# Retention output of a two-block layer stack, computed with tokens on partitions instead of features

## The reference

```
for layer in range(DEPTH_2):
    h = rms_norm(x, pre_norm[layer])
    proj = h @ w_in[layer]          # c_b c_c c_x c_z r_q r_k r_v r_z
    ...
    q, k = rotary(r_q), rotary(r_k)
    scores[i, j] = (q_i . k_j) * decay(i - j) / sqrt(128)      (j <= i)
    ret_i = sum_j scores[i, j] * v_j            # written in chunks of 128 tokens
    ret = ret * rsqrt(mean(ret * ret, axis=-1) + 1e-6)         # per token and head
    y_ret = ret * silu(r_z)
    out = concat(y_conv, y_ret) @ w_out[layer]
    x = x + rms_norm(out, post_norm[layer])
```

## Time and profile before

| | |
|---|---|
| median of 3 runs | 2066.09 us (2065.78 to 2068.53) |
| the profiled execution | 2066.39 us, its span in the trace 2064.6 us |
| mean granted TensorE clock | 0.975 of full speed |
| busy: PE, DVE, ACT, POOL | 95%, 55%, 32%, 3% of the span |
| weight loads (PEld) | 84% of the span |
| DMA | 165.52 MB, 80 GB/s over the span |

### The profile page before, as it was taken

The page is one execution under the profiler, slowest core; times in us unless marked ns, Lnnn a source line. Parts: engine busy times, 40 slices in busy tenths (PEclk is TensorE's granted clock), DMA queues, the critical chain, the costliest instruction groups (busy, mean ns, idle before and its releaser), DMA issues.

```text
span 2064.6 us, 30485 instructions
## 1 busy us (share of the span) xinstructions
PE 1969.5 (95%) x11905; PEld 1732.4 (84%) x11905; DVE 1132.6 (55%) x1481; ACT 661.8 (32%) x960; POOL 65.9 (3%) x67
## 2 busy tenths in 40 slices
PE   6999999998989999999799999999978999999997
PEld 6998888888989989989578888888857888888886
DVE  6777786786645535555654554445245555445422
ACT  3123344344324525324422222222222222222222
POOL 1000000001000000000000000000000000000000
PEclk8999999999999999999899999999989999999999
DMA  4221111111222232322222321332222222233231
GB/s 137 94 82 60 44 61 41 61 41 62 82 82 82 81 102 81 102 82 66 77 72 92 91 91 61 102 102 85 98 61 71 91 91 74 78 97 95 92 102 41
DMA packets 159194, 165.52 MB, mean 80 GB/s; under 512 B 2969, under 2 KB 156066, under 8 KB 159155
## 3 DMA queue, kind: packets, MB, share of 16 engines
q1 hardware_dynamic: 156648, 160.73, 24.4%
q10 hardware_dynamic: 2186, 4.20, 0.6%
q0 software_dynamic: 320, 0.07, 0.0%
HBM read 162.88 MB, written 2.10 MB: 80 GB/s over the span
## 4 chain that ended last, share of the span: by engine, by line
PE 53%; issue 40%; DVE 3%; ACT 2%; POOL 1%; DVEq 0%; DMA 0%; ACTq 0%; POOLq 0%
PE acc L373 44%; PE acc L675 2%; PE acc L477 1%; PE tr L709 1%; PE tr L408 1%; POOL pw L315 1%; PE sc L398 1%; PE sc L695 1%; PE tr L549 0%; DVE h L1484 0%; PE sc L515 0%; ACT w_hi L774 0%; DVE ssum L1496 0%; PE tr L547 0%; PE sc L408 0%
## 5 line engine op out<-in xcount | busy, mean ns | idle before, releaser
L1103 DVE TENSOR_TENSOR w_lo<-raw,w_hi 128x2048 fp32r<-128x2048 f32 x150 | 343.2, 2288 | 175.4 <-ACT w_hi L774 173.6
L774 ACT ACTIVATE w_hi<-raw 128x2048 fp32r<-128x2048 f32 x149 | 284.5, 1911 | 355.2 <-PE acc L373 354.5
L373 PE MATMUL acc<-s_lo,w_hi 128*128 128x512 f32 x896 | 359.6, 401 | 19.2 <-DVE s_lo L1488 13.0
L373 PE MATMUL acc<-s_hi,w_lo 128*128 128x512 f32 x896 | 352.8, 394 | 0.0
L373 PE MATMUL acc<-s_hi,w_hi 128*128 128x512 f32 x896 | 352.7, 394 | 0.0
L373 PE MATMUL acc<-n_lo,w_hi 128*128 128x256 f32 x1600 | 339.7, 294 | 12.5 <-DVE n_lo L1131 6.2
L373 PE MATMUL acc<-n_hi,w_hi 128*128 128x256 f32 x1600 | 328.8, 287 | 0.0
L373 PE MATMUL acc<-n_hi,w_lo 128*128 128x256 f32 x1600 | 328.7, 287 | 0.0
L373 PEld LDWEIGHTS acc<-n_lo,w_hi 128*128 128x128 f32 x1600 | 253.2, 191 | 25.2 <-issue 19.9
L373 PEld LDWEIGHTS acc<-n_hi,w_lo 128*128 128x128 f32 x1600 | 254.4, 191 | 0.0
L373 PEld LDWEIGHTS acc<-n_hi,w_hi 128*128 128x128 f32 x1600 | 254.3, 191 | 0.0
(11 more groups left out here) (247 smaller groups left out, 2438.3 us busy)
## 6 DMA issues: line engine op xcount, KB each, us to landing
raw<-in_w_in SPq DMA_DIRECT2D x92, 1024.0 KB, 5.4
raw<-in_w_up SPq DMA_DIRECT2D x22, 1024.0 KB, 5.0
raw<-in_w_out SPq DMA_DIRECT2D x20, 1024.0 KB, 4.9
raw<-in_w_down SPq DMA_DIRECT2D x8, 1024.0 KB, 5.0
raw<-in_w_conv_out SPq DMA_DIRECT2D x4, 1024.0 KB, 5.0
decay<-in_decay ACTq DMA_DIRECT2D x8, 512.0 KB, 3.4
raw<-in_w_down SPq DMA_DIRECT2D x4, 768.0 KB, 4.2
xs<-in_x SPq DMA_DIRECT2D x4, 512.0 KB, 5.3
```

The lines of the kernel that those rows point to most:

```text
L373: last = pe.matmul(acc[jj][:, bank, at_:at_ + n], w[j][:, k, jj * P:(jj + 1) * P], x[:, k0 + k, c:c + n], start=start and k == 0 and p == ...
L774: act.activation(w_hi[j][:, :, :], raw[j][:, :, :], ACT.Copy).then_inc(hi_full[j], 1)
L1103: dve.tensor_tensor(w_lo[j][:, :, :], raw[j][:, :, :], w_hi[j][:, :, :].bitcast(fp32), ALU.subtract).then_inc(lo_full[j], 1)
```

## The change

The roles in retain are exchanged: the decayed scores are stationary in blocks of 128x128, v moves, and the output has tokens on partitions and features along the free dimension. The two heads go to different halves of the PSUM tile tr (ret_at), so the copy into rq between them goes away. The squares' sums over features are now sums along the free dimension: ScalarE squares each block of 128 and adds up in the same instruction (accum_out into es). The reciprocal root of a token is then a value per partition, and VectorE scales the output straight from PSUM into rq. To get back to features on partitions, TensorE transposes four blocks a head (turn) into sc, and VectorE multiplies those by the gate. The column sums and the broadcast leave the loop, and with them their semaphores' counts (bc_l in place of st_l, not shown).

More of the change, by code:

```diff
@@ L74 @@
 LAY_ST = 6
+LAY_BC = 2
 ST_END = ST_LAY + LAYERS * LAY_ST
+BC_END = ST_LAY + LAYERS * LAY_BC
 KINDS = [None, 0, 1, 2, 3]
@@ L190, in build, with st_at, ret_at @@
         tr = ctx.enter_context(nc.psum_tensor("tr", [P, 2, 512], fp32))
+        def st_at(kb):
+            return kb * SEQ - P * (kb * (kb - 1) // 2)
+        def ret_at(hh):
+            return tr[:, 1 - hh, :]
         def scores_at(kb):
@@ L213, in build @@
             "ret_done cy0_full cconv cm_full ch_full c_done post ld_pos o_tr o_cp ss_zero mean_v "
-            "wo_half retm ld_decay trig cpad prep").split()}
+            "wo_half retm ld_decay trig cpad prep turned").split()}
         block = ctx.enter_context(nc.Block())
@@ L651, in _ @@
                 st_l = l * LAY_ST + ST_LAY
+                bc_l = l * LAY_BC + ST_LAY
                 pe.wait_ge(s["ss_full"], l * (2 * KT) + 3 * KT)
@@ L688, in scores_t @@
                             pe.wait_ge(s["qk_full"], l * 16 + i * 4 + 4)
-                            pe.wait_ge(s["rb_full"], st_l + i + 2)
+                            pe.wait_ge(s["rb_full"], bc_l + 2)
                         else:
@@ L1012, in _ @@
                 f_l = l * LAY_F + 2 * B_LAY
-                st_l = l * LAY_ST + ST_LAY
+                bc_l = l * LAY_BC + ST_LAY
                 hi(0, b_l, (acc_full[1], f_l))
                 hi(1, b_l, (acc_full[1], f_l))
-                rstd(st_l, [tr], 0)
+                rstd(bc_l, [tr], 0)
                 for t in range(KT):
@@ L1022, in _ @@
                     square(l * (2 * KT) + 3 * KT, t, h[:, t, META:], (s["h_full"], l * KT + (t + 1)), width=SEQ)
-                act.wait_ge(s["st_bc"], st_l + 2)
+                act.wait_ge(s["st_bc"], bc_l + 2)
                 act.activation(rp[:, :], tr[:, 0, :], ACT.Copy).then_inc(s["rb_full"], 1)
@@ L1034, in _, with square_sums @@
                                   src=acc[jj][:, 0, :])
-                    def copy_ret(hh):
+                    def square_sums(hh):
                         act.wait_ge(s["ro_psum"], hd0 + hh + 1)
-                        act.activation(sq[:, hh, 0:SEQ], tr[:, 1, :], ACT.Square).then_inc(s["ret"], 1)
-                        act.activation(rq[:, hh, :], tr[:, 1, :], ACT.Copy).then_inc(s["ro_full"], 1)
+                        for q in range(NQT):
+                            last = act.activation(sq[:, hh, q * P:(q + 1) * P], ret_at(hh)[:, q * P:(q + 1) * P],
+                                                  ACT.Square, accum_out=es[:, hh, q:q + 1])
+                        last.then_inc(s["ret"], 1)
                     hi_for(0, b1 + 2, f1 + 4)
-                    copy_ret(0)
-                    copy_ret(1)
+                    square_sums(0)
+                    square_sums(1)
                     for jj in range(2):
@@ L1469, in _ @@
                 ss_l = l * (2 * KT) + 3 * KT
-                mean_square(st_l, 4, 1.0 / D, 1e-6)
+                bc_l = l * LAY_BC + ST_LAY
+                mean_square(bc_l, 4, 1.0 / D, 1e-6)
                 start_sum(0)
@@ L1473, in _ @@
                 dve.wait_ge(s["h_zero"], 2)
-                dve.wait_ge(s["rb_full"], st_l + 1)
+                dve.wait_ge(s["rb_full"], bc_l + 1)
                 for t in range(KT + 2):
@@ L1496, in _ @@
                     dve.tensor_tensor(ssum[:, 0:SEQ], ssum[:, 0:SEQ], sq[:, t % 2, 0:SEQ], ALU.add).then_inc(s["ss_full"], 1)
-                mean_square(st_l + 1, 4, 1.0 / D, 1e-6)
+                mean_square(bc_l + 1, 4, 1.0 / D, 1e-6)
                 lo(1, b_l)
@@ L1544, in _ @@
                     lo(0, b1 + 2)
-                    dve.wait_ge(s["rb_full"], st_l + 2)
+                    dve.wait_ge(s["rb_full"], bc_l + 2)
                     scale_z(0)
-                    dve.wait_ge(s["st_sum"], st_l + i + 3)
-                    dve.tensor_tensor(head_ms[:, :], sc[:, 0, 0:8], pp2[:, :], ALU.mult).then_inc(s["hv"], 1)
+                    dve.wait_ge(s["ret"], hd0 + 2)
+                    dve.tensor_tensor(head_ms[:, :], es[:, :, :].rearrange("p a n -> p (a n)"), pp2[:, :],
+                                      ALU.mult).then_inc(s["hv"], 1)
                     dve.wait_ge(s["hv"], l * 4 + i + 1)
@@ L1636, in _ @@
             weigh(0, 3)
-            mean_square(ST_END, 4, 1.0 / D, 1e-6)
+            mean_square(BC_END, 4, 1.0 / D, 1e-6)
             weigh(3, KT)
```

## The result

The changed kernel takes 2109.4 us (median, 2109.21 to 2110.49), the kernel before 2067.11 us in the same comparison (2065.78 to 2068.53). The ratio is 1.0206, with a 95% interval of 1.0188 to 1.0223: 42 us slower, 10 of them more than the sum had.

The account below looks back on a forecast made before the run. TensorE's own queue was taken to bound the retention loop, eight passes of about 56.5 us. Queue gain -20.6, waits +41.2 and clock +11.7 made +32.3 us, so 2098 us, with 8 in 10 for 2086 to 2111.

Parts of the forecast that it names:

- the sum: Over eight passes of the retention loop: -20.6 + 41.2 + 11.7 = +32.3 us, given as 2098 us.
- The queue's gain: TensorE's queue in the loop: sums and broadcast leave, small matmuls and transposes enter; -2.6 us a pass, -20.6 over eight.
- The wait before K: End of each pass: TensorE waits for VectorE to free acc0 behind turn(1); 5.2 or 5.0 us, 41.2 over eight.
- turn(0) costs nothing: Head 0's transposes don't wait for VectorE's scaled output, being covered by queued matmuls with about 4 us left.
- The clock: Behind each wait before K, TensorE runs one stretch at 0.50, losing 1.5 us; 8 x 1.5 = 11.7 us.
- (a): Rival: the wait before K is there but the clock doesn't fall; +20.6, 2087 us; chance 0.09.
- (b): Rival: behind the wait the clock stays down longer, or waits come out longer; +3.0 a pass, 2110 us; chance 0.13.
- the case of one short stretch: Main case: one wait of about 5 us and one slow stretch a pass; 2090 to 2106 us; chance 0.68.
- (c): Rival: TensorE's transposes or small matmuls cost more than their trace spacing; 1.5 a pass for transposes, 2110 us; chance 0.05.
- (d): Rival: K doesn't wait because VectorE frees acc0 in time; only the queue's gain stays, 2045.5 us; chance 0.05.

Follow-up runs that it names:

- both turns together: The changed kernel with the transposes of both heads placed together behind the first tile of Q; 2046.77 us, ratio 0.990 to the kernel before.
- filled version: The changed kernel with 22 useless matmuls of 512 columns between the second turn and K; 2090.17 us, ratio 1.011 to the kernel before.
- turns in the middle of a tile: The changed kernel with both turns behind step four of eight of Q's first tile, gate multiplies ahead of lo; 2047.23 us, ratio 0.9901.
- half filled: The changed kernel with 11 useless matmuls between the second turn and K; 2096.86 us, ratio 1.0134 to the kernel before.
- four steps ahead: The changed kernel with head 1's transposes four steps (12 matmuls) ahead of the end of Q's second tile; 2081.31 us, ratio 1.0061.
- the wait alone: The kernel before, VectorE edited only: head 1's gate multiply waits for both Q tiles, lo made ahead of the multiplies; 2128.75 us, ratio 1.0294.

## Why the prediction was right, point by point

- **The queue's gain.** The forecast was 2.6 us a pass. ScalarE's first copy of v is at 1177.81 and 1234.37 in the kernel before, 56.56 us a pass, and a pass without a wait (both turns together) is 54.00: 2.56 us. The output matmuls of a head, from the changed kernel's timeline, 1078.15 to 1080.31, take 2.16 us against 2.07 and a forecast of 2.12:

```profile
1078.15 2.40 PE L719 MATMUL tr<-rv,st 128*128 128x128 f32 x20
1080.31 0.48 PE L383 MATMUL acc<-s_lo,w_hi 128*128 128x512 f32 x1
```

- **The wait before K.** Forecast 5.2 and 5.0, measured 5.08 to 5.11 and 4.87; 41.2 against 40.3 us. The brackets count from the modelled end of the last record. Counted as the forecast did, from the moment at which K could have issued (1102.20 + 0.35 = 1102.55), the first wait is 5.35, and a pass of the filled version is just that much longer than one without a wait, 59.35 against 54.00. So the sum was a little low here, not high. That it comes from the place of the second turn is shown by four kernels: moved away, it goes; moved by six and by twelve matmuls, it shrinks to 3.7 and 2.3; put into the kernel before, it comes there.
- **turn(0) costs nothing.** No wait stands before it: GpSimd was done with the power at 1089.19, VectorE with the scaled output of both heads at 1092.91, and head 0's turn issued at 1096.27: 3.4 us to spare, against a forecast of about 4.
- **The clock is the term that was mis-sized.** The step was "I take one such stretch a pass: 8 x 1.5 = 11.7 us". In the changed kernel all eight stretches are 6.7 us at 0.50, and 4.8 to 5.6 us of each fall on matmuls; the filled wait prices them at 2.4 us a pass (19 us), which is 7 of the 10 us that the sum lacked. The passes say the same: 1250.77 - 1189.17 = 61.60 us between two copies of v, less the 59.35 of the filled version, whose K starts as late, is 2.25; over the six passes it is 2.2 to 2.6. What led me wrong was taking the length of the stretch from waits of 1.9 and 3.1 us. The trace of the kernel before has a wait of 4.41 us behind dense matmuls, in the first block, and the clock is at 0.50 for 6.7 us there. I didn't use it. The wait nearest in length, 5.09 us until 1018.14, would not have helped, since the clock is at 0.50 before that wait begins:

```profile
510.01 0.78 PE L373 MATMUL acc<-n_lo,w_hi 128*128 128x256 f32 x2 [4.41 <-DVE n_lo L1336]
...
509.10:515.80 6.70, 5.79 (x26) 0.50 0.00 0
...
1012.00:1013.00 1.00, 1.00 (x5) 0.50 0.00 0
```

- **The remainder.** The spans differ by 43.1 us. The first copy of v in the loop is 0.8 us late (1065.52 against 1064.69), and a ScalarE instruction behind the last pass is 41.65 late (1841.26 against 1799.61), so 40.8 us come in between, nearly all of them from the eight passes (8 x 5.1). The 0.8 is a balance of parts outside the change: the changed kernel loses 1.3 us before 898 us and 1.5 in a stretch at 0.50 from 902 to 905 us, and lacks a stretch that the kernel before has at 1058.7. The last 1.5 us are lost at the very end, where the changed kernel's clock is at 0.50 for 6.7 us (2089.8 to 2096.5) and that of the kernel before for 3.3 (2048.5 to 2051.8). That any of this has to do with the change isn't shown.
- **The rivals.** (a) is refuted: the clock fell at each of the eight waits. (b) was what happened to the clock, at 2.4 of its 3.0 us: I gave it 0.13, and 0.68 to the case of one short stretch. The measured 2109.4 lies outside the 2090 to 2106 of that case and inside 2086 to 2111 only because that range took in (b). (c) is refuted by the run without transposes (0.84 us a pass for eight) and by the 2.16 us of the output matmuls. (d), the gain without the wait, isn't what this change does, but 2045.5 was right for it: a kernel with both turns behind Q's first tile has 2046.8.

By the Trainium skill's 275 ns a transpose ("TensorE: Matmul & The Clock Gate", Part 4, PE-mode transpose) the sum would have been an estimated 2110. That is near the measured 2109.4, and for the wrong reason: the runs put a transpose at about 0.1 us of the queue.

The best version that the experiments found is the one with both turns together, from which the one with turns in the middle of a tile can't be told apart: 1% below the kernel before, from the changed kernel by moving one call of four transposes.

## What to carry to other kernels

Ask of each instruction that is put into a full queue not what it takes but who now waits for it, and what stands behind that wait on the other engine. The transposes cost 0.8 us a pass, and the place of half of them cost 7.6: the multiply that waited for them stood in VectorE's queue ahead of the operation that freed TensorE's next accumulator. Where a product alternates between few PSUM tiles, work handed to another engine belongs at least one whole tile ahead of the tile's reuse. And a wait on TensorE should be priced with the clock behind it, here nearly half as much again.

## What the runs showed of the hardware

- The fall of the clock behind a wait isn't a function of its length alone. Waits of 3.08 us (kernel before, second layer) and, in four of eight cases, of 2.35 to 2.59 us (half filled) left it at 1.00, while all eight of 2.1 to 2.4 us (four steps ahead) were followed by a stretch at 0.50. The same wait of 1.94 us at a loop's start was followed by such a stretch in the kernel before and by none in the changed one (1.00 from 1059.5 to 1065.0).
- Waits of 3.5 to 3.7 us were followed by 3.4 or by 6.8 us at 0.50. Those of 4.9 to 5.1 in the changed kernel were always followed by about 6.7, of which 4.8 to 5.6 fell on matmuls; of the eight as long in the kernel before with the wait alone, two were followed by 3.4 only.
- Matmuls whose result nobody reads made the kernel 19 us faster than an idle TensorE did.
- Four transposes of 128x128 fp32 take 0.35 us of TensorE's queue in the middle of other matmuls (0.42 by the run without them, which counts the slower issue behind them), and 20 records of 128 columns with fresh weights 2.16 us, 0.108 each.
